# Chunk 2 of a Strassen-style up-projection made paired, and weight splits ahead of the bank work in the down-projection

## Chip, cores and metric

One core of one Trainium2 chip. The metric is the device time of one execution in microseconds (us); lower is better. The kernel before was timed in three runs, and one further execution was profiled.

## What is computed

A decoder layer on 512 tokens of width 2048: attention groups and an output projection, then a feed-forward part. The change touches only the feed-forward part:

```python
def conv_glu_ffn(h, w_up, conv_w, conv_b, w_down):
    u = h @ w_up                                   # (512, 2048) @ (2048, 11264)
    c = conv_general_dilated(u, conv_w, ...) + conv_b   # causal, depthwise, width 3
    gate, val = jnp.split(c, 2, axis=-1)
    return (jax.nn.gelu(gate, approximate=True) * val) @ w_down   # (5632, 2048)
```

All matrices are float32. A RMS norm stands before and after, and the result is added to x.

## The kernel before

**Products in two parts.** Every operand is split into a high part (rounded to float32r, by ScalarE: `hp_to_hi`, `half_to_hi`, `item_to_hi`) and a low part (operand minus high part, by VectorE: `hp_to_lo`, `item_to_lo`, L1884 and L1899). TensorE adds hi x hi, hi x lo and lo x hi in PSUM.

**Up-projection.** The product is done by a seven-product scheme (Strassen-Winograd): the tokens and the inner dimension are halved, gate and value columns are the two halves of the third. The 5632 columns of each half are handled in 22 chunks of 256. Each chunk has seven products P1, P2, P6, P5, P7, P3, P4 (in that order), each in two halves f of 128 columns, so 14 half products, each of 8 k-tiles. `SEQ` lists them; half product w uses slot w % 4 of the split weights `hp_hi` and `hp_lo`. The right operands are quarters of w_up (B11, B12, B21, B22) and their sums T1 = B11 + B12, T2 = T1 + B22, T3 = B12 + B22, T4 = T2 + B21 (signs are taken up elsewhere). P6 takes T2, P5 takes T1, P7 takes T3, P4 takes T4.

**Unpaired and paired chunks.** In an unpaired chunk TensorE issues three 256-wide matmuls for each k (`three_more`, L2509). In a paired one (`two`, L2503) the left operand's high and low parts lie side by side and stream as one 512-wide matmul against the weights' high part; a 256-wide matmul with the low part follows. A paired chunk fills banks 512 wide, so ScalarE's copies out of them (`snap_paired`) are twice as wide, and VectorE must add the two halves (`fold`, and `c12`). Chunks 3 to 20 are paired (`PAIRED`, L77).

**Who makes the sums.** Where a chunk is unpaired, VectorE adds all of T1 to T4 (`make_t`, L1602); T1 and T2 of chunk 2 are made at the last two half products of chunk 1, T3 and T4 in chunk 2. From `PAIRED[0]` on, POOL (GpSimd) issues three adding transfers for each chunk (L1076 to L1088): T1 once the low part of P1's second half is done and B12 has landed, then T3, then T4. VectorE makes T2 alone, at the first half product of the chunk, and waits there for T1's transfer. This goes on to the last chunk, 21, although that one is unpaired.

**Around a half product.** After half product (or half step) w, ScalarE and VectorE each run `after(w)` in program order: bank copies or subtractions, the split of weights w + 4 into the slot just freed, then convolution, gelu, product and left sums of the chunk before, a few instructions for each w. SP's queue loads quarters and stores the products of the chunk before (`spill`, `spill_sums`).

**Down-projection.** Four passes over 22 pairs of row blocks of w_down, two half steps for each pair. Passes 0 and 1 have 12 matmuls, 512 wide, in either half step; passes 2 and 3 have 12 and 6. Each pass adds up in its own set of PSUM banks over all its steps. `w_at(v)` (L788) is the last half step but one of pass v. At the pass boundaries the banks are emptied: ScalarE's `keep` (L1348) copies four banks after `w_at(0)` and `w_at(1)` and two after the next half step; VectorE's `sum_f` (L2084) combines banks and copies, six sums after `w_at(v) + 1` and two more (`12c`) later in the same `after`; after `w_at(2)` two sums, then eight. TensorE's `bank_free` (L2572) waits for these copies and sums before it begins a bank again. In the kernel before they stand at the head of `after`, ahead of the weight split. `item_to_hi` and `item_to_lo` split left operands that were stored and loaded back.

**VectorE also makes block sums** of the down-projection's weights (L1918, `sums_a`; L1909, `sums_b` and `sum_t4`), each ahead of a low part in `after`.

Of the kernel before, what the change touches and what calls it, by code (L numbers as in the profile page):

```python
# [73 lines left out]
CHUNKS = FT // 2  # L74
N_PROD = 7
HPS = 2 * N_PROD
PAIRED = range(3, CHUNKS - 1)  # L77
H_DOWN = CHUNKS * HPS
N_PAIRS = FT // 2
N_PASS = 4  # L80
# [338 lines left out]
def build(nc, x, mem, rel_bias, w_in, a_sinks, w_mem_kv, w_out, g_mix_post, w_up, w_down, g_ffn_post,  # L419
# [13 lines left out]
    with ExitStack() as ctx:  # L433
# [354 lines left out]
        def w_at(v):  # L788
            return H_DOWN + 2 * N_PAIRS * v + 2 * N_PAIRS - 2
# [302 lines left out]
        def _(act):  # L1092
# [172 lines left out]
            for u in range(U_FFN - 1):  # L1265
                for r in range(4):
# [5 lines left out]
                    if (u, r) in SQUARE_AT:  # L1272
                        what, t = SQUARE_AT[u, r]
# [10 lines left out]
                    n = acc_evacuated(u, r)  # L1284
# [198 lines left out]
            def after(w):  # L1483

                c, p, f = SEQ[w] if w < H_DOWN else (CHUNKS, w % HPS // 2, w % 2)
                s = 2 * p + f
                act.wait_ge(hp_used, w + 1)
                if w in (w_at(0), w_at(1)):
                    for what in ("12", "21"):
                        for m in range(2):  # L1490
                            keep(w == w_at(1), what, m)
                if w in (w_at(0) + 1, w_at(1) + 1):
                    for m in range(2):
                        keep(w == w_at(1) + 1, "11", m)
                if c < CHUNKS:
                    if p in SNAP_OF and not (c == 1 and p == P1):
                        (snap_paired if c in PAIRED else snap)(c, SNAP_OF.index(p), f)
                    if c == 0 and p == P7:
                        snap(1, 0, f)
                if w == 3:  # L1500
                    for pair in TURN_H[1]:
                        h_from_psum(1, pair)
                    hp_to_hi(6)
                    hp_to_hi(7)
                elif 3 < w < H_DOWN - 4:
                    hp_to_hi(w + 4)
                elif w >= H_DOWN - 4:
                    half_to_hi(w + 4 - H_DOWN)
                if w == 4:
                    sum_to_hi(OP_S2, 0)  # L1510
                    sum_to_hi(OP_S2, 1)
                if w == 6:
                    sum_to_hi(OP_S1)
                if w == 7:
                    sum_to_hi(OP_S3)
                if w == 9:
                    sum_to_hi(OP_S4)
                if w == 10:
                    sum_to_hi(OP_A22)
                if w == 11:  # L1520
                    act.wait_ge(left_lo, LEFT_COUNT[-1])
                    for f in range(2):
                        act.wait_ge(c11_done, f + 1)
                        act.activation(u_gate[:, f, 0:HALF_S], snaps[:, 0, f, :], ACT.Copy).then_inc(c11_kept, 1)
                i = conv_at(w, c, s)
                if 0 < c <= CHUNKS:
                    if i == 0:
                        if c == 2:
                            begin_conv(c - 1, 0, 0)
                        begin_conv(c - 1, 0, 1)  # L1530
                    if i in (2, 3):
                        gelu(c - 1, i - 2)
                if c < CHUNKS:
                    if s in (12, 13):
                        begin_conv(c, 1, s - 12)
                    if s == 13 and c != 1:
                        begin_conv(c, 0, 0)
                for i in ITEMS_AT.get(w, []):
                    item_to_hi(i)
                if w >= w_at(2) + 4 and w < w_at(2) + 12 and w % 2 == 0:  # L1540
                    f_square(0, (w - w_at(2) - 4) // 2)

# [39 lines left out]
        def _(dve):  # L1582
# [236 lines left out]
            for u in range(U_FFN - 1):  # L1819
                for r in range(4):  # L1820
# [24 lines left out]
                    n = acc_evacuated(u, r)  # L1845
# [27 lines left out]
                    if U_OUT <= u < U_SPLIT and (u - U_OUT) % 4 == 3:  # L1873
                        c = (u - U_OUT) // 4
# [241 lines left out]
            def after(w):  # L2116
# [1 line left out]
                c, p, f = SEQ[w] if w < H_DOWN else (CHUNKS, w % HPS // 2, w % 2)  # L2118
                s = 2 * p + f
                dve.wait_ge(hp_used, w + 1)  # L2120
                if w == w_at(0) + 1 or w == w_at(1) + 1:
                    for m in range(2):
                        for what in ("12b", "21a", "22a"):
                            sum_f(w == w_at(1) + 1, what, m)
                if w == w_at(2):
                    sum_f(0, "11", 0)
                    sum_f(0, "11", 1)
                if w == w_at(2) + 1:
                    sum_f(0, "21b", 0)
                    sum_f(0, "21b", 1)  # L2130
                if w == 14:
                    make_t(1, "T2")
                if PAIRED[0] <= c < CHUNKS and s == 0:
# [49 lines left out]
                if c < CHUNKS:  # L2183
                    if s == 5 and c < PAIRED[0]:
                        make_t(c, "T4")
                    if c == 1 and s in (12, 13):
                        make_t(c + 1, ("T1", "T2")[s - 12])
                    if c == 2 and s == 0:
                        make_t(c, "T3")
                    if s == (5 if c in PAIRED else 10) and c > 0:  # L2190
                        for half in range(2):
# [7 lines left out]
                for i in ITEMS_AT.get(w, []):  # L2199
                    item_to_lo(i)  # L2200
                if w == w_at(0) + 1 or w == w_at(1) + 1:
                    for m in range(2):
                        sum_f(w == w_at(1) + 1, "12c", m)
                if w == w_at(2) + 1:
                    for m in range(2):
                        for what in ("12", "22", "21"):
                            sum_f(0, what, m)
# [453 lines left out]
```

## Time and profile before

| | |
|---|---|
| median of 3 runs | 2003.32 us (2002.27 to 2005.06) |
| the profiled execution: its time | 2007.25 us |
| its span, first to last instruction | 2005.4 us |
| granted TensorE clock, mean | 0.999 of full speed |
| busy: TensorE, VectorE, ScalarE, POOL | 98%, 74%, 50%, 3% |
| chain that ended last, by engine | TensorE 82%, VectorE 11%, issue 3%, ScalarE 3%, DMA 1% |
| up-projection | 668 us to 1562 us of the span, roughly |
| down-projection | 1562 us to 1987 us, roughly |

The times that the profile gives are positions in the span. A timeline row has start, length, engine, line, operation and tiles, then a count (x2 where two like instructions were merged) and in brackets the idle time before it with what ended it. Matmuls are pipelined: the length of one overlaps the next, and the distance between two starts is what one costs.

### The profile page before, as it was taken

The page shows a single profiled execution, that of the slowest core. Times are in us where ns is not written, and L with a number is a line of the kernel's source. Part 1 is how long each engine was busy: PE and PEld are TensorE (multiplying, and loading weights), DVE is VectorE, ACT ScalarE, POOL GpSimd, SP SyncE. Part 2 cuts the span into 40 slices and gives each one's busy share as a digit, 9 for nine tenths or more (in the row PEclk, how much of TensorE's full clock was granted, in tenths as well). Part 3 has the DMA queues.
Part 4 walks back from the last instruction along what each step waited for, and adds up shares of the span by engine and source line. Part 5 has one row for each costly group of instructions (what it writes and reads, how often), then busy time and mean ns, then how long its engine had stood idle before and what let it go on. Part 6 is the DMA issues. An engine that isn't in the chain of part 4 may idle for free.

```text
span 2005.4 us, 27812 instructions
## 1 busy us (share of the span) xinstructions
PE 1969.9 (98%) x10408; PEld 1678.8 (84%) x10408; DVE 1475.8 (74%) x2046; ACT 1011.8 (50%) x1538; POOL 50.3 (3%) x63
## 2 busy tenths in 40 slices
PE   8999999999999999999999999999999999999997
PEld 6888888888887889888888888888889888887885
DVE  4343544545446999788888888888888998879888
ACT  6442332435435755555555555555555655554454
POOL 0000000000000000000000000000000000000000
PEclk9999999999999999999999999999999999999999
DMA  9463222211646444787777877787777997877685
GB/s 384 150 223 95 93 90 71 77 64 64 252 127 213 165 137 153 192 202 220 213 196 201 232 201 199 205 229 203 197 208 196 308 312 233 293 242 233 203 275 189
DMA packets 229109, 388.03 MB, mean 193 GB/s; under 512 B 11842, under 2 KB 139970, under 8 KB 219120
## 3 DMA queue, kind: packets, MB, share of 16 engines
q1 hardware_dynamic: 219520, 320.19, 47.6%
q0 software_dynamic: 8208, 59.77, 14.8%
q10 hardware_dynamic: 1248, 6.29, 0.8%
q8 instruction: 83, 1.36, 0.3%
q14 instruction: 50, 0.41, 0.1%
HBM read 286.30 MB, written 44.07 MB: 165 GB/s over the span
## 4 chain that ended last, share of the span: by engine, by line
PE 82%; DVE 11%; issue 3%; ACT 3%; DMA 1%; SPq 0%; DVEq 0%; ACTq 0%
PE ring L2505 15%; PE ring L2261 12%; PE ring L2263 12%; PE ring L2262 12%; PE ring L2507 8%; PE side L2505 7%; PE side L2507 3%; DVE w_lo L1897 3%; PE side L2261 2%; PE side L2262 2%; PE side L2263 2%; PE side L2337 1%; PE side L2310 1%; DVE f L2107 1%; PE side L2320 1%
## 5 line engine op out<-in xcount | busy, mean ns | idle before, releaser
L1596 DVE TENSOR_TENSOR w_lo<-raw,w_hi 128x512 fp32r<-128x512 f32 x256 | 169.6, 688 | 270.2 <-ACT w_hi L1115 270.0
L2505 PE MATMUL ring<-s,w_hi 128*128 128x512 f32 x864 | 308.1, 400 | 2.4 <-ACT snaps L1434 2.3
L1897 DVE TENSOR_TENSOR w_lo<-raw,w_hi 128x1024 fp32r<-128x1024 f32 x216 | 253.4, 1173 | 74.5 <-ACT w_hi L1325 55.0
L1897 DVE TENSOR_TENSOR w_lo<-q,w_hi 128x1024 fp32r<-128x1024 f32 x218 | 255.5, 1173 | 46.2 <-ACT w_hi L1325 27.9
L1115 ACT ACTIVATE w_hi<-raw 128x512 fp32r<-128x512 f32 x256 | 151.1, 622 | 197.9 <-PE ring L2263 193.5
L2507 PE MATMUL ring<-s,w_lo 128*128 128x256 f32 x864 | 242.9, 281 | 0.0
L1325 ACT ACTIVATE w_hi<-q 128x1024 fp32r<-128x1024 f32 x176 | 185.0, 1055 | 52.4 <-PE side L2507 46.8
L2505 PE MATMUL ring<-a,w_hi 128*128 128x512 f32 x576 | 204.4, 399 | 0.0
L2261 PE MATMUL ring<-w_hi,act_hi 128*128 128x512 f32 x488 | 192.9, 395 | 9.2 <-DVE w_lo L1596 8.7
L2505 PEld LDWEIGHTS ring<-s,w_hi 128*128 128x128 f32 x864 | 162.4, 188 | 44.8 <-ACT snaps L1434 4.9
L1325 ACT ACTIVATE w_hi<-raw 128x1024 fp32r<-128x1024 f32 x130 | 135.1, 1056 | 114.9 <-DVE raw L1600 78.4
L2262 PE MATMUL ring<-w_lo,act_hi 128*128 128x512 f32 x488 | 190.8, 391 | 0.0
L2263 PE MATMUL ring<-w_hi,act_lo 128*128 128x512 f32 x488 | 190.7, 391 | 0.0
L2507 PEld LDWEIGHTS ring<-s,w_lo 128*128 128x128 f32 x864 | 163.5, 189 | 0.0
L2507 PE MATMUL ring<-a,w_lo 128*128 128x256 f32 x576 | 162.0, 281 | 0.0
L2261 PE MATMUL ring<-act_hi,w_hi 128*128 128x512 f32 x384 | 155.3, 404 | 0.0
L2263 PE MATMUL ring<-act_hi,w_lo 128*128 128x512 f32 x384 | 150.3, 391 | 0.0
L2262 PE MATMUL ring<-act_lo,w_hi 128*128 128x512 f32 x384 | 149.6, 390 | 0.0
L1336 ACT ACTIVATE w_hi<-raw 128x1024 fp32r<-128x1024 f32 x86 | 82.6, 960 | 96.1 <-PE ring L2263 46.4
L1336 ACT ACTIVATE w_hi<-q 128x1024 fp32r<-128x1024 f32 x86 | 82.4, 960 | 96.3 <-PE ring L2263 41.5
L2505 PEld LDWEIGHTS ring<-a,w_hi 128*128 128x128 f32 x576 | 108.3, 188 | 26.8
L2261 PEld LDWEIGHTS ring<-w_hi,act_hi 128*128 128x128 f32 x488 | 92.1, 189 | 29.7 <-issue 8.5
(329 smaller groups left out, 4359.5 us busy)
## 6 DMA issues: line engine op xcount, KB each, us to landing
q<-in_w_up SPq DMA_DIRECT2D x65, 1024.0 KB, 5.6
raw<-in_w_in SPq DMA_DIRECT2D x24, 1024.0 KB, 5.2
raw<-in_w_up SPq DMA_DIRECT2D x23, 1024.0 KB, 8.1
q<-q POOLq DMA_DIRECT2D x19, 1024.0 KB, 6.9
q<-raw POOLq DMA_DIRECT2D x19, 1024.0 KB, 6.9
raw<-q POOLq DMA_DIRECT2D x19, 1024.0 KB, 7.3
q<-in_w_down SPq DMA_DIRECT2D x66, 256.0 KB, 4.7
raw<-in_w_down SPq DMA_DIRECT2D x66, 256.0 KB, 4.5
```

The lines of the kernel that those rows point to most:

```text
L1115: act.activation(w_hi[:, s, r * QTR:(r + 1) * QTR], raw[:, s, r * QTR:(r + 1) * QTR], ACT.Copy).then_inc(hi_done, 1)
L1325: act.activation(hp_hi[:, h % 4, :].rearrange("p (k n) -> p k n", n=P), hp_source(h), ACT.Copy, scale=-1.0 if p == P1 else 1.0).then_inc(h ...
L1336: act.activation(half_at(e)[0], half_source(e), ACT.Copy).then_inc(hp_hi_done, 1)
L1596: dve.tensor_tensor(w_lo[:, s, q], raw[:, s, q], w_hi[:, s, q].bitcast(F32), ALU.subtract).then_inc(lo_done, 1)
L1897: dve.tensor_tensor(lo, src, hi.bitcast(F32), ALU.subtract).then_inc(hp_lo_done, 1)
L2107: dve.tensor_tensor(dst, a, b, op).then_inc(f_summed, 1)
L2261: pe.matmul(dst, a_hi_, b_hi_, start=first, stop=False)
L2262: pe.matmul(dst, a_hi_, b_lo_, start=False, stop=False)
L2263: return pe.matmul(dst, a_lo_, b_hi_, start=False, stop=last)
L2310: pe.matmul(score_ps[score_bank(n)][:, 0:nk * P], q_place(n), keys[:, k0 * P:(k0 + nk) * P], start=True, stop=True).then_inc(scores_ready, 1)
L2505: pe.matmul(bank.rearrange("p (h n) -> p h n", h=2), b_hi, hi_lo, start=first, stop=False, skip_group_check=True)
L2507: return pe.matmul(bank[:, 0:HALF_S], b_lo, hi_lo[:, 0, :], start=False, stop=last, skip_group_check=True)
```

## The change

Chunk 2 joins the paired chunks, so its T1, T3 and T4 are made by POOL's transfers, and VectorE makes only its T2, at its first half product. In the down-projection, ScalarE's copies out of the banks (`keep`) and VectorE's sums (`sum_f`) move from the head of `after` to behind the split of the next weights and the left operands.

```diff
-PAIRED = range(3, CHUNKS - 1)
+PAIRED = range(2, CHUNKS - 1)
...
@@ ScalarE, after(w)
                 act.wait_ge(hp_used, w + 1)
-                if w in (w_at(0), w_at(1)):
-                    for what in ("12", "21"):
-                        for m in range(2):
-                            keep(w == w_at(1), what, m)
-                if w in (w_at(0) + 1, w_at(1) + 1):
-                    for m in range(2):
-                        keep(w == w_at(1) + 1, "11", m)
                 if c < CHUNKS:
...
                 for i in ITEMS_AT.get(w, []):
                     item_to_hi(i)
+                if w in (w_at(0), w_at(1)):
+                    for what in ("12", "21"):
+                        for m in range(2):
+                            keep(w == w_at(1), what, m)
+                if w in (w_at(0) + 1, w_at(1) + 1):
+                    for m in range(2):
+                        keep(w == w_at(1) + 1, "11", m)
...
@@ VectorE, after(w)
                 dve.wait_ge(hp_used, w + 1)
-                if w == w_at(0) + 1 or w == w_at(1) + 1:
-                    for m in range(2):
-                        for what in ("12b", "21a", "22a"):
-                            sum_f(w == w_at(1) + 1, what, m)
-                if w == w_at(2):
-                    sum_f(0, "11", 0)
-                    sum_f(0, "11", 1)
-                if w == w_at(2) + 1:
-                    sum_f(0, "21b", 0)
-                    sum_f(0, "21b", 1)
...
-                    if c == 1 and s in (12, 13):
+                    if c == 1 and s in (12, 13) and c + 1 < PAIRED[0]:
                         make_t(c + 1, ("T1", "T2")[s - 12])
-                    if c == 2 and s == 0:
+                    if c == 2 and s == 0 and c < PAIRED[0]:
                         make_t(c, "T3")
...
                 for i in ITEMS_AT.get(w, []):
                     item_to_lo(i)
                 if w == w_at(0) + 1 or w == w_at(1) + 1:
+                    n = w == w_at(1) + 1
                     for m in range(2):
-                        sum_f(w == w_at(1) + 1, "12c", m)
+                        for what in ("12b", "21a", "22a"):
+                            sum_f(n, what, m)
+                    sum_f(n, "12c", 0)
+                    sum_f(n, "12c", 1)
+                if w == w_at(2):
+                    sum_f(0, "11", 0)
+                    sum_f(0, "11", 1)
                 if w == w_at(2) + 1:
+                    sum_f(0, "21b", 0)
+                    sum_f(0, "21b", 1)
                     for m in range(2):
                         for what in ("12", "22", "21"):
                             sum_f(0, what, m)
```

## Rows read from the trace of the kernel before

**Rows 1.** The page: TensorE's busy time, and its granted clock in 40 slices.

```profile
PE 1969.9 (98%) x10408; PEld 1678.8 (84%) x10408; DVE 1475.8 (74%) x2046; ACT 1011.8 (50%) x1538; POOL 50.3 (3%) x63
...
PEclk9999999999999999999999999999999999999999
```

**Rows 2.** TensorE's waits: released by; us in total, times, longest us.

```profile
PE side L2261 <- DVE w_lo L1897: 3.4, 3, 1.3
PE ring L2505 <- ACT snaps L1434: 2.3, 6, 0.8
...
PE side L2261 <- DVE f L2107: 0.8, 1, 0.8
```

**Rows 3.** TensorE's timeline: chunk 2's start and wait, starts of chunks 3, 4, 21.

```profile
764.33 0.28 PE L2511 MATMUL ring<-a,w_hi 128*128 128x256 f32 x1
764.45 0.28 PE L2512 MATMUL ring<-a,w_hi 128*128 128x256 f32 x1
...
781.49 0.28 PE L2513 MATMUL ring<-s,w_lo 128*128 128x256 f32 x1
781.98 0.38 PE L2511 MATMUL ring<-s,w_hi 128*128 128x256 f32 x1 [0.21 <-ACT snaps L1455]
...
805.11 0.40 PE L2505 MATMUL ring<-a,w_hi 128*128 128x512 f32 x1
...
844.68 0.40 PE L2505 MATMUL ring<-a,w_hi 128*128 128x512 f32 x1
...
1521.90 0.28 PE L2511 MATMUL ring<-a,w_hi 128*128 128x256 f32 x1
```

**Rows 4.** VectorE's timeline: P1's second low parts (chunks 2, 3), T2 and P6.

```profile
761.45 1.22 DVE L1894 SCALAR_TENSOR_TENSOR w_lo<-q,w_hi 128x1024 fp32r<-128x1024 f32 x1
...
800.99 1.23 DVE L1894 SCALAR_TENSOR_TENSOR w_lo<-q,w_hi 128x1024 fp32r<-128x1024 f32 x1 [0.99 <-ACT w_hi L1325]
...
809.81 2.29 DVE L1600 TENSOR_TENSOR raw<-raw,q 128x2048 f32<-128x2048 f32 x1 [1.74 <-DMA q<-q]
813.29 1.23 DVE L1897 TENSOR_TENSOR w_lo<-raw,w_hi 128x1024 fp32r<-128x1024 f32 x1 [1.19 <-ACT w_hi L1325]
```

**Rows 5.** T1's transfers (line 1079), and a window: busy by engine, clock, DMA, GB/s.

```profile
DMA to landing us min/median/max: 6.8/6.9/8.0
...
764.00:768.00 4.00, 4.00 (x36) 4.00 (x35) 4.00 (x5) 2.86 (x4) 0.00 (x0) 1.00 0.39 137
```

**Rows 6.** Timelines at the first pass boundary: ScalarE, VectorE, TensorE.

```profile
1680.08 1.09 ACT L1352 ACTIVATE f<-side 128x512 f32<-128x512 f32 x2 [1.61 <-PE ring L2263]
...
1682.00 1.08 ACT L1336 ACTIVATE w_hi<-raw 128x1024 fp32r<-128x1024 f32 x1
...
1684.33 0.68 DVE L2107 TENSOR_TENSOR f<-side,f 128x512 f32<-128x512 f32 x1
...
1688.18 1.22 DVE L1918 TENSOR_TENSOR q<-q 128x1024 f32<-128x1024 f32 x1
...
1688.32 0.51 PE L2261 MATMUL side<-w_hi,act_lo 128*128 128x512 f32 x1 [0.80 <-DVE f L2107]
```

**Rows 7.** The same at the second pass boundary.

```profile
1800.89 1.09 ACT L1352 ACTIVATE f<-side 128x512 f32<-128x512 f32 x2 [2.04 <-PE ring L2263]
...
1804.50 1.10 ACT L1352 ACTIVATE f<-ring 128x512 f32<-128x512 f32 x2
...
1805.94 0.69 DVE L2107 TENSOR_TENSOR f<-side,f 128x512 f32<-128x512 f32 x1
...
1812.79 1.22 DVE L1897 TENSOR_TENSOR w_lo<-raw,w_hi 128x1024 fp32r<-128x1024 f32 x1
...
1814.07 0.50 PE L2261 MATMUL side<-w_hi,d_tok 128*128 128x512 f32 x1 [1.29 <-DVE w_lo L1897]
```

**Rows 8.** The same at the third: VectorE, TensorE.

```profile
1894.64 1.29 DVE L2107 TENSOR_TENSOR f<-ring,f 128x512 f32<-128x512 f32 x2 [0.51 <-PE ring L2263]
...
1905.45 0.50 PE L2261 MATMUL side<-w_hi,d_tok 128*128 128x512 f32 x1 [1.31 <-DVE w_lo L1897]
```

## The prediction

> **What bounds the kernel now.** I read the page first, then TensorE's waits, and last the timeline around each place that the diff touches. The page puts TensorE at 98% busy, and its granted clock stands in the top tenth in all forty slices [rows 1], so it runs at its level of 2.4 GHz. What counts is therefore how fast TensorE can issue, and where it stands still. Its standstills in the FFN are few [rows 2]: 2.3 us in six waits for ScalarE's bank copies (paired chunks), 3.4 us in three waits for weights' low parts, and 0.8 us in one wait for a bank sum (both in the down-projection). The change can win only what these rows and the streams themselves hold. A measurement of this kernel can tell about 0.2%, 4.0 us, from no change.
>
> **Part 1: chunk 2 becomes paired.** The streams. An unpaired half product issues 8 times three 256-wide matmuls, a start every 0.12 us (764.33 to 764.45), so 0.36 us for each k. A paired one issues a 512-wide and a 256-wide matmul. A chunk has 14 half products of 8 k, 112 in all. Unpaired that is 112 x 0.36 = 40.32 us. Paired, chunk 3 ran from 805.11 to 844.68, 39.57 us or 0.3533 for each k [rows 3]. Gain 0.75 us.
> By the Trainium skill (TensorE: Matmul & The Clock Gate, Back-to-back issue gap) a warm matmul of N columns follows its predecessor after N/2.4 + 2.5 ns. Its estimate would be 327.5 ns against 324.9 ns for each k, a gain of 0.3 us, and the total would come out 0.5 us higher. The rows disagree with it (120 ns where it says 109), and the sum goes by the rows.
>
> The wait inside chunk 2. TensorE stood at 781.49 to 781.98, 0.37 us over its pitch, for a bank copy, and the restart cost 0.1 more. The whole chunk took 805.11 - 764.33 = 40.78 us, 1.21 more than chunk 3. I take all **1.21** off: the first paired chunk of the trace had hardly a wait.
>
> What the later chunks do. The 18 paired chunks took (1521.90 - 805.11) / 18 = 39.82 us each, 0.25 over the clean one [rows 3]. Chunk 3 moves from first paired to second, so I give it the mean: **+0.25** (ends 0 and 0.9, the longest wait of that kind in rows 2 with its restart).
>
> The sums by transfers. VectorE loses T1, T3 and T4 of chunk 2, three times 2.29 us [rows 4]. It gains 256 columns more in six subtractions, six folds and two additions of halves, which I put at zero to 7 us of VectorE by the 0.68 us of a 512-wide pass [rows 6]. No wait of rows 2 for VectorE lies in an up-projection chunk of either kind, so both are worth nothing on the path. ScalarE's six bank copies go from 256 to 512 wide; chunk 3 carries the same and did not wait. If that cover fails, the price is the 0.25 just booked.
>
> What is new on the path is T1's transfer. POOL issues it once the second half of chunk 2's P1 has its low part. VectorE waits for it to make T2, T2 is split by ScalarE and VectorE, and then TensorE takes it as P6. Behind T2 in VectorE's order stand that split and the conv taps of chunk 1; behind the transfer in POOL's queue stand T3's and T4's. In chunk 3 this chain is in the rows [rows 4]: trigger at 800.99, T2 begins at 809.81 (8.82 later, 1.74 of it idle for the DMA), the low part of P6's weights begins at 813.29 (3.48 later) and lasts 1.23. Together 13.53 us. In chunk 2 the trigger stands at 761.45, so the weights are ready at 774.98. TensorE comes to P6 after four half products, 764.33 + 32 x 0.3533 = 775.64. Slack: 0.65 us. In chunk 3 the trigger came 4.1 us before the chunk, here 2.9, so the slack is thinner than anywhere in the trace. Against it: the stores of chunk 0's products run between 764 and 768, a DMA share of 0.39 of 4 us, which is 1.56 us of all engines [rows 5], while in chunk 3 the queues were empty. And one of 19 such transfers took 8.0 us where the median took 6.9 [rows 5], 1.1 more. So the stall lies between 0 and 1.56 + 1.1 - 0.65 = 2.0 us; queueing in full without the slow transfer gives 0.9, none gives 0. I take **+0.4**, between those two, as the stores overlap only the transfer's front.
> The Trainium skill (DMA: Bandwidth & Descriptors, Anatomy of one DMA) gives a POOL-issued transfer as 2.0 us + bytes / 436e3, estimated 4.4 us for this megabyte; with it the stall would be 0 and the total 0.4 us lower. The trace's median for the adding transfer is 6.9, so the rule is not followed here.
>
> Removing T1 and T2 from the end of chunk 1 relieves VectorE there, where no row shows TensorE waiting: 0. The loads of chunks 3 and 4 that waited for T4 now wait for the transfer, as in chunk 3, and there it hurt nothing: 0.
>
> **Part 2: weights before the sums, at three pass boundaries.** Call S the last half step but one of a pass. ScalarE's order after S was four bank copies, weights, two copies, weights; it becomes weights, four copies, weights, two copies. VectorE's sums (0.6 to 0.65 us each) move behind one block sum and one low part.
> First boundary [rows 6]: today ScalarE copies from 1680.08 and splits at 1682.00, VectorE's six sums run from 1684.33 to 1688.18, and TensorE restarts at 1688.32. It waits for the last of those sums, not for weights. In the new order the first split and the four copies end at 1680.08 + 0.95 + 1.92 = 1682.95, the next split starts there, its low part starts 1.2 later and lasts 1.2, and the sums begin at 1685.3. The block sum fits in idle time. All is 1.0 later: **+1.0**.
> Second boundary [rows 7]: from 1805.94 VectorE works without a gap through six sums, a block sum and a low part (1.2), two more sums and a block sum up to the low part at 1812.79, for which TensorE restarts at 1814.07. In the new order ScalarE's second split starts at 1804.50 (the last two copies' present place), its 512-wide low part ends at about 1805.75, and what follows is the chain without those 1.2 us: 6.85 - 1.2 = 5.65. The low part begins at 1805.75 + 5.65 = 1811.4, **-1.4**. The first bank copy now ends 0.95 + 0.74 + 0.49 = 2.2 us after S, behind the split and the part of a left operand that stands between 1800.89 and 1804.50; TensorE comes to that bank a half step after S, 12 matmuls or 2.7 us: hidden, with 0.5 to spare, and a cost of the difference if an item more stood there.
> Third boundary [rows 8]: VectorE works without a gap from 1894.64, S's end, to TensorE's restart at 1905.45. The amount of work stays, but in the new order the first thing after one 0.6 us block sum is a low part that ScalarE delivers 1.2 after S: 0.6 us of idle enters a full chain, **+0.6**. The bank sums it pushes back make TensorE wait earlier instead.
> Together +0.2. Ends: -4.2 if the two last waits of rows 2 go altogether (3.4 + 0.8), +1.6 if the second boundary gives nothing. I take the worked-out value. SP's loads wait for low parts, which come earlier, or 0.6 later at the third. But the block sum that now stands ahead of the bank sums needs its blocks up to 5.4 us sooner (1688.18 becomes 1682.8), and no row of mine shows them landed; VectorE would stand in that wait with low part and sums queued behind it. I price it at 0 and put the rest into (b).
>
> **Sum.** -1.21 + 0.25 + 0.4 + 0.2 = **-0.4 us**. The profiled execution took 2007.25 us (span 2005.4 and 1.85 around it), so it would take 2006.9. It lies 3.9 above the median of the runs, 2003.32, and against that I forecast **2002.9**.
>
> **Rivals.**
> (a) Slower: T1's transfer is late. Place: P6 of chunk 2; it decides once T1 lands more than 0.65 us later than in chunk 3's rhythm. With the full 2.0 us: -1.21 + 0.25 + 2.0 + 0.2 = +1.2, 2004.5. For: the thin slack and the stores. Against: the stores begin over 2 us after the trigger, and they fill only 0.39 of their window. 0.2.
> (b) The sums behind the weights cost at the first and third boundary and give nothing at the second, because its block sum waits there for a load that came in time only for the old place: -1.21 + 0.25 + 0.4 + 1.6 = +1.0, 2004.4. For: the first boundary's wait is for a sum. Against: VectorE's gapless chain at the second. 0.13.
> (c) Faster: the boundary waits all go, -4.8, 1998.6. For: the long waits name low parts. Against: VectorE's work between S and the restart hardly shrinks. 0.05.
> My forecast has 0.58; 0.04 is for what no row shows.
>
> **Range.** From the forecast down with no T1 stall (0.4), no waits in chunk 3 (0.25) and one boundary wait gone (1.3), less about 0.7 for the scatter of a median (runs: 2002.27 to 2005.06): 2000.2. Upward (a) with the same scatter: 2005.2. All cases but (c) and a part of the unseen stay within 4.0 us: same 0.91, faster 0.05, slower 0.04.
>
> **What would show it.** Chunk 2 should take about 40.0 us on TensorE, with three POOL transfers in it; T2 waiting 1 to 3 us for the DMA, and the step is wrong if TensorE waits over 1 us at P6. The wait at the first boundary should grow to about 1.8 us for a sum, the second should keep one wait of about 1 us, and the third should split into two short ones. I am wrong altogether if chunk 2 does not shorten, or if the waits of rows 2 go without others in their place.

## The result, and the profile after

The changed kernel is slower, by a little: 2007.64 us median (2004.61 to 2011.28, 20 runs) against 2004.12 us (2001.54 to 2006.64, 20 runs) for the kernel before. The ratio is 1.0019 with a 95% interval of 1.0013 to 1.0025. The forecast was 2002.9 with a range of 2000.2 to 2005.2, so it was wrong in direction and outside the range: -0.4 us was forecast as the change and +3.5 came (a further 0.8 of the distance is that 20 runs of the kernel before have a higher median than the three of the forecast). The profiled execution took 2009.72 us, 2.5 more than the one of before.

The page of the changed kernel, the lines that answer to [rows 1], and one from its part on DMA queues (packets, MB, share of 16 engines):

```profile
span 2007.9 us, 27595 instructions
PE 1969.7 (98%) x10296; PEld 1672.9 (83%) x10296; DVE 1474.7 (73%) x2051; ACT 1013.8 (50%) x1538; POOL 52.9 (3%) x66
...
PEclk9999999999999999999999999999999999999999
...
q8 instruction: 82, 1.34, 0.3%
```

The clock is granted in full as before, and TensorE has 112 matmuls fewer. The time is not in its work but between it. TensorE's waits of the changed kernel, first in the up-projection's chunks from 2 on, then in the down-projection (us in total, times, longest):

```profile
PE ring L2504 <- ACT snaps L1434: 6.9, 7, 2.0
PE ring L2504 <- DVE w_lo L1897: 0.5, 3, 0.2
...
PE side L2260 <- DVE w_lo L1897: 1.5, 2, 1.0
PE side L2260 <- DVE f L2107: 1.4, 2, 1.0
PE ring L2260 <- DVE f L2107: 1.2, 2, 0.8
PE ring L2260 <- DVE w_lo L1897: 0.3, 1, 0.3
```

Against [rows 2] the waits for bank copies grew from 2.3 us to 6.9, while those of the down-projection went from 5.3 (1.1 of it in two waits that are not among the rows shown) to 4.4. TensorE's lines carry a number one lower than before, and one or more higher in some of the kernels below. So the loss lies in the up-projection. Stretches of the changed kernel there, each from one chunk's first matmul to the next chunk's: chunks 2, 3, 6 and 8 (length, then busy time by engine, clock, DMA share, GB/s):

```profile
764.74:807.16 42.42, 40.17 (x227) 34.31 (x225) 33.26 (x42) 22.36 (x29) 2.61 (x3) 1.00 0.80 214
807.16:848.37 41.21, 39.65 (x226) 34.25 (x225) 33.70 (x44) 21.72 (x28) 2.59 (x3) 1.00 0.76 201
928.15:967.72 39.57, 39.57 (x226) 34.30 (x225) 33.83 (x44) 21.73 (x28) 2.59 (x3) 1.00 0.79 210
1007.29:1048.93 41.64, 39.99 (x227) 34.28 (x226) 33.83 (x44) 21.72 (x28) 2.59 (x3) 1.00 0.75 200
```

The kernel before, chunks 2, 3 and 8:

```profile
764.33:805.11 40.78, 40.57 (x339) 40.37 (x338) 36.53 (x40) 21.28 (x29) 1.02 (x1) 1.00 0.44 146
805.11:844.68 39.57, 39.57 (x227) 34.33 (x226) 32.06 (x41) 21.72 (x28) 2.61 (x3) 1.00 0.79 210
...
1004.32:1044.37 40.05, 39.82 (x226) 34.35 (x225) 33.84 (x44) 21.72 (x28) 2.61 (x3) 1.00 0.77 207
```

A clean chunk with wide operands takes 39.57 us in both. Chunk 2 became 1.6 us longer instead of 0.8 shorter. More striking, chunks 3, 8 and 13 (39.98 to 40.66), whose code the diff does not touch, lost 1.6, 1.6 and 0.7, and chunks 6, 7, 12 and 17, which took 40.1 to 40.7, are now clean. The balance is 2.8 us from chunk 2's start to the up-projection's last matmul (797.8 to 800.6 us). One profiled execution of each kernel is compared here, and executions differ: `down_only` below has the same instructions as the kernel before up to the end of the up-projection and took 795.7 us for this stretch, with chunks 7, 12 and 17 at 39.7, 39.6 and 39.6. What comes back from trace to trace is chunk 2 (42.42 us here, 42.44 in `up_only`, 42.60 in `after_pad224`) and chunk 8 (40.1 us in both traces with the stream of before, 41.6 in the changed kernel, `up_only` and `sums_by_vector`).

**Where TensorE's wait in chunk 2 comes from.** The changed kernel's timeline around chunk 2, by engine (VectorE, POOL, VectorE, ScalarE, TensorE):

```profile
761.88 1.22 DVE L1894 SCALAR_TENSOR_TENSOR w_lo<-q,w_hi 128x1024 fp32r<-128x1024 f32 x1
...
763.41 1.01 POOL L1079 DMA_DIRECT2D q<-q  x1 [761.95 <-DVE w_lo L1894]
...
771.59 2.29 DVE L1600 TENSOR_TENSOR raw<-raw,q 128x2048 f32<-128x2048 f32 x1 [3.49 <-DMA q<-q]
775.07 1.22 DVE L1897 TENSOR_TENSOR w_lo<-raw,w_hi 128x1024 fp32r<-128x1024 f32 x1 [1.19 <-ACT w_hi L1325]
777.98 1.23 DVE L1897 TENSOR_TENSOR w_lo<-raw,w_hi 128x1024 fp32r<-128x1024 f32 x1 [1.69 <-ACT w_hi L1325]
...
781.71 0.74 DVE L2059 SCALAR_TENSOR_TENSOR c_gate<-u_gate,conv,c_gate 128x511 f32<-128x511 f32 x1
782.49 0.75 DVE L2062 SCALAR_TENSOR_TENSOR c_gate<-u_gate,conv,c_gate 128x510 f32<-128x510 f32 x1
...
783.27 0.63 ACT L1411 ACTIVATE c_gate<-c_gate 128x512 f32<-128x512 f32 x1 [1.00 <-DVE c_gate L2062]
783.81 0.58 ACT L1434 ACTIVATE snaps<-ring 128x512 f32<-128x512 f32 x1
...
776.44 0.47 PE L2504 MATMUL ring<-s,w_hi 128*128 128x512 f32 x1 [0.23 <-DVE w_lo L1897]
...
784.44 0.50 PE L2504 MATMUL ring<-s,w_hi 128*128 128x512 f32 x1 [2.02 <-ACT snaps L1434]
```

Read upward from the last row. TensorE stands for 2.02 us at product P5, until ScalarE has copied the bank of P6 (783.81). That copy stands in ScalarE's order behind the second gelu of chunk 1 (783.27), which waited 1.00 us for VectorE's taps (781.71, 782.49). The taps stand behind the low parts of P6's weights (775.07, 777.98), these behind T2 (771.59), and T2 waited 3.49 us for T1's transfer (763.41). The row at 776.44 is the wait that I had priced: TensorE at P6, 0.23 us for the low part, 0.4 us with the restart, which is what I had put down. The 2.02 us at P5, some 2.3 us with the restart, are another branch of the same chain: the late transfer reaches TensorE a second time, through T2, the low parts and the taps on VectorE, then the gelu and the copy on ScalarE.

**Why T1 is late in chunks 3 and 8.** POOL's issues of T1 and T3 in the changed kernel, in chunk 3 and in a clean chunk; T3 (L1083) is issued as soon as T1 has landed:

```profile
804.73 0.89 POOL L1079 DMA_DIRECT2D q<-q  x1 [24.37 <-DVE w_lo L1894]
814.40 0.87 POOL L1083 DMA_DIRECT2D q<-raw  x1 [8.79 <-DMA q<-q]
...
886.15 0.86 POOL L1079 DMA_DIRECT2D q<-q  x1 [24.30 <-DVE w_lo L1894]
893.58 0.86 POOL L1083 DMA_DIRECT2D q<-raw  x1 [6.57 <-DMA q<-q]
```

From issue to issue it is 9.67 us in the one and 7.43 in the other. What moved between these moments, by the DMA view of the changed kernel (804.73 to 814.40, then 886.15 to 893.58):

```profile
q0 software_dynamic: 144, 1.05, 52.9%
q8 instruction: 1, 0.02, 0.6%
...
q0 software_dynamic: 144, 1.05, 68.4%
```

The same 144 packets in both, and in the slow one a single packet of instructions. I compared the T1 transfers of all thirteen traces (the kernels before and after and the eleven below), except those of chunk 2, beside which stores run. In 149 of them no packet of the two instruction queues, q8 and q14, started between the issue and the next issue: all took 7.39 to 7.65 us. In the other 98 one did: 7.40 to 9.71 us. No transfer over 7.65 was without one. Queue q8 holds TensorE's instructions: a kernel below with 1029 instructions more on TensorE alone has 4 packets more on it. One such packet comes for every 257 or so of TensorE's instructions, that is at a place set by counting. The change takes 224 instructions out of chunk 2 and so moves every later packet of q8. Not all the chunks that changed follow q8: in chunk 6 of the kernel before T1 took 8.11 us with a packet of q14 alone beside it.

The packets' own times say more about the longest ones. Such a transfer is 128 packets of 8 KB and, at its end, 16 of 4 bytes. In 24 transfers a packet of q8 started 6.9 to 7.1 us behind the issue. In 17 of them it started no earlier than the last of the 4-byte packets, and they took 7.55 to 8.24 us. In the other seven the last 4-byte packet started as the 16 KB packet ended (7.9 to 8.1 us behind the issue, within 0.02 us of that end), and they took 9.61 to 9.71. Chunk 3 of the changed kernel is one of the seven: fetch from 7.07 to 8.05, last packet at 8.04 where a clean transfer has it at 6.49.

The down-projection's three boundaries in the changed kernel, TensorE's restarts that answer to [rows 6 to 8]:

```profile
1690.59 0.50 PE L2260 MATMUL side<-w_hi,act_lo 128*128 128x512 f32 x1 [0.48 <-DVE f L2107]
1692.51 0.50 PE L2260 MATMUL side<-w_hi,act_lo 128*128 128x512 f32 x1 [0.96 <-DVE f L2107]
...
1816.92 0.50 PE L2260 MATMUL side<-w_hi,d_tok 128*128 128x512 f32 x1 [0.99 <-DVE w_lo L1897]
...
1900.54 0.50 PE L2260 MATMUL ring<-w_hi,d_res 128*128 128x512 f32 x1 [0.34 <-DVE f L2107]
1903.03 0.47 PE L2260 MATMUL ring<-w_hi,d_res 128*128 128x512 f32 x1 [0.84 <-DVE f L2107]
```

### The profile page after: what moved, and what is told of

It is laid out like the page before. It is cut to its first block, busy times and chain, and to the rows that moved or that the text cites. A ratio compares the mean times of both kernels' runs of the same rounds, so it can differ in the third digit from the quotient of the medians.

```text
span 2007.9 us, 27595 instructions
## 1 busy us (share of the span) xinstructions
PE 1969.7 (98%) x10296; PEld 1672.9 (83%) x10296; DVE 1474.7 (73%) x2051; ACT 1013.8 (50%) x1538; POOL 52.9 (3%) x66
## 3 DMA queue, kind: packets, MB, share of 16 engines
q8 instruction: 82, 1.34, 0.3%
## 4 chain that ended last, share of the span: by engine, by line
PE 83%; DVE 10%; ACT 3%; issue 2%; DMA 2%; DVEq 0%; ACTq 0%; SPq 0%
PE ring L2504 15%; PE ring L2260 12%; PE ring L2262 12%; PE ring L2261 12%; PE ring L2506 8%; PE side L2504 7%; PE side L2506 3%; DVE w_lo L1897 3%; PE side L2260 2%; PE side L2261 2%; PE side L2262 2%; PE side L2336 1%; PE side L2309 1%; DMA q<-q 1%; DVE f L2107 1%
## 5 line engine op out<-in xcount | busy, mean ns | idle before, releaser
L2504 PE MATMUL ring<-s,w_hi 128*128 128x512 f32 x912 | 324.6, 399 | 7.4 <-ACT snaps L1434 6.9
L2506 PE MATMUL ring<-s,w_lo 128*128 128x256 f32 x912 | 255.9, 281 | 0.0
L2504 PE MATMUL ring<-a,w_hi 128*128 128x512 f32 x608 | 215.3, 398 | 0.0
L2504 PEld LDWEIGHTS ring<-s,w_hi 128*128 128x128 f32 x912 | 171.3, 188 | 52.6 <-ACT snaps L1434 10.0
L2506 PEld LDWEIGHTS ring<-s,w_lo 128*128 128x128 f32 x912 | 172.2, 189 | 0.0
L2506 PE MATMUL ring<-a,w_lo 128*128 128x256 f32 x608 | 170.6, 281 | 0.0
L2504 PEld LDWEIGHTS ring<-a,w_hi 128*128 128x128 f32 x608 | 114.2, 188 | 28.2
```

The lines of the kernel that those rows point to most:

```text
L2504: pe.matmul(bank.rearrange("p (h n) -> p h n", h=2), b_hi, hi_lo, start=first, stop=False, skip_group_check=True)
L2506: return pe.matmul(bank[:, 0:HALF_S], b_lo, hi_lo[:, 0, :], start=False, stop=last, skip_group_check=True)
```

## The experiments

**Which half.** `up_only` is the kernel before with chunk 2's edits alone:

```
-PAIRED = range(3, CHUNKS - 1)
+PAIRED = range(2, CHUNKS - 1)
...
-                    if c == 1 and s in (12, 13):
+                    if c == 1 and s in (12, 13) and c + 1 < PAIRED[0]:
-                    if c == 2 and s == 0:
+                    if c == 2 and s == 0 and c < PAIRED[0]:
```

> The kernel before with the up-projection's part of the change alone (chunk 2 paired, its T1, T3, T4 by transfers). Theory A (the loss is T1's transfer, which comes late for chunk 2 and holds up VectorE's taps, ScalarE's gelu and with it the copy of P6's bank): nearly the whole loss, +2.5 to +4 us against before, with chunk 2 at 41.5 to 42.5 us. Rival C (the loss is in the down-projection's new order): 0 to +1 us here. Rival B (the wider copies and folds are what is late): also +2.5 to +4, told apart by the kernel with the sums on VectorE.

It took 2007.21 us (ratio 1.0016, interval 1.0007 to 1.0025). Its chunks 2, 3 and 8 took 42.44, 41.66 and 41.63 us, and its waits for bank copies, 6.8 us in seven, the longest 2.0, are those of the changed kernel.

`down_only` is the rest of the diff (the keeps and sums behind the weights).

> The kernel before with the down-projection's part of the change alone (weights ahead of the bank work). Theory A: the same as before within 0.5 us, the waits being +1.0, -1.4 and +0.5 us at the three pass boundaries as in the trace after. Rival C: +2.5 to +4 us.

2004.69 us, ratio 1.0003 (0.9994 to 1.0012). Its chunks 2, 3 and 8 take 40.80, 39.57 and 40.06 us, as before. It cannot be told from the kernel before, and `up_only` can: the loss that the runs resolve is in the first half.

**Chunk 2's sums back on VectorE.** In `sums_by_vector` chunk 2 keeps wide operands, and T1 to T4 of it are made by VectorE; POOL starts with chunk 3:

```
+BY_DMA = 3
-            for c in range(PAIRED[0], CHUNKS):
+            for c in range(BY_DMA, CHUNKS):
```

> The kernel after, but chunk 2's T1 to T4 are made by VectorE where they were before (T1 and T2 at the end of chunk 1); chunk 2 stays paired and the transfers begin with chunk 3. Theory A: no wait at P5 of chunk 2, which takes 39.6 to 39.9 us; in all 1 us under before and 4 to 5 us under after. Rival B (wider copies and folds): chunk 2 keeps a wait of about 2 us, and the time stays near after's.

2006.57 us, ratio 1.0015 (1.0006 to 1.0023): the gain did not come. Chunk 2 took 40.72 us and not the 39.6 to 39.9 expected, with one wait of 0.8 us for the copy: VectorE's own T3 stands ahead of the taps here. It lost the wait of 2 us, so wide copies and folds are not what made that one; they stand in every clean chunk of 39.57 us too. And chunk 3, with the first transfer, took 42.61:

```profile
PE ring L2505 <- ACT snaps L1435: 4.9, 5, 1.5
PE ring L2505 <- DVE w_lo L1898: 1.1, 1, 1.1
```

The lateness moved on by one chunk: chunk 3's T1 was issued 0.7 us before the chunk's start, where 2.3 to 2.6 is usual, and took 8.92 us, with a packet of q8 in it. Chunk 8 stayed at 41.59, so its trouble does not come from who makes chunk 2's sums.

**The link through the gelu.** `gelu_later` is the changed kernel with ScalarE's two gelus one product later, so that a gelu that waits for its taps no longer stands ahead of P6's copy:

```
-                    if i in (2, 3):
-                        gelu(c - 1, i - 2)
+                    if i in (3, 4):
+                        gelu(c - 1, i - 3)
```

> The kernel after with ScalarE's two gelus one half product later (behind the copy of P6's first bank instead of ahead of it). Theory A (the link from T1 to TensorE runs through the second gelu): the waits at P5 go in chunks 2 to 20 except for what still reaches the first gelu; every chunk near 39.6 us, the up-projection 5 to 7 us shorter than after's, and the whole 4 to 7 us under after, 1 to 3 under before. A rival in which T1 holds up TensorE by the weights of P6 alone: nothing changes, within 0.5 us of after.

2003.45 us, ratio 0.9994 (0.9985 to 1.0003), about 4 us under the changed kernel. No wait for a copy is left; where T1 is late, P6 itself waits for its weights (chunk 3 still takes 41.15 us, chunk 2 only 40.35):

```profile
PE ring L2504 <- DVE w_lo L1897: 3.2, 6, 1.4
```

`before_gelu_later` makes the same edit in the kernel before.

> The kernel before with ScalarE's two gelus of a chunk one product later. The chain that I hold for the lost time is: late T1, late weights of product 6, VectorE's taps of the convolution behind them, ScalarE's second gelu behind the taps, the copy of TensorE's bank behind the gelu, TensorE at product 5. In this kernel a gelu that waits no longer stands ahead of that copy, so the excess of chunks 4, 6, 7, 8, 12, 13, 17 and 18 (3.4 us in all over 39.57) should go down to under 1 us: 2000.5 to 2002.0 us. If the excess was not in this link but in the weights of product 6 themselves: 2004.1 us.

2002.57 us, ratio 0.9990 (0.9981 to 0.9999), 0.6 us above the range that I gave. In the profile the 18 chunks from 3 to 20 take 39.57 us each, with no wait at all. The windows view over them:

```profile
805.36:1517.68 712.32, 712.32 (x4035) 617.73 (x4033) 606.82 (x772) 395.35 (x504) 46.81 (x54) 1.00 0.79 209
```

The kernel before took 716.79 us for them [rows 3: 805.11 to 1521.90], so the link cost 4.5 us in that execution already, and 2.4 in that of `down_only` (714.73 us). The ratio of the times says 2 us.

**The chain's slack, directly.** `late_t1` is the kernel before with POOL waiting for the weights of P2's first bank:

```
-                pool.wait_ge(hp_lo_done, place(c, P1, 1) + 1)
+                pool.wait_ge(hp_lo_done, place(c, P2, 0) + 1)
```

> The kernel before with T1's start delayed: POOL waits for VectorE's weights of product 2's first bank in place of product 1's second, about 2.6 us later. By the chain through the taps, the gelu and the bank's copy, whose slack is 0.15 to 0.35 us, TensorE pays nearly all of it at product 5: each of the 18 chunks with wide operands grows from 39.57 to about 41.8 us, some 40 us in all, 2044 us. By the slack of 1.9 us that my prediction read at product 6's weights it would pay only 0.7 us per chunk, some 13 us in all, 2017 us.

2051.98 us in one run, past the 2044 expected by the chain through the copy and far from the 2017 of the other. The 18 chunks took 758.85 us, 42.16 each, where a clean one takes 39.57: 2.6 us of delay cost 2.6 on average, and 2.0 to 2.6 in the 13 chunks whose T1 took 7.4 to 7.6 us. In chunk 5, T2 waits 3.40 us for the transfer, and TensorE pays at two places, P6's weights and P6's copy. First TensorE's waits of this kernel, then the two restarts of that chunk:

```profile
PE ring L2505 <- ACT snaps L1434: 24.9, 17, 1.5
PE ring L2505 <- DVE w_lo L1897: 16.1, 18, 2.0
...
904.04 0.47 PE L2505 MATMUL ring<-s,w_hi 128*128 128x512 f32 x1 [0.48 <-DVE w_lo L1897]
911.33 0.50 PE L2505 MATMUL ring<-s,w_hi 128*128 128x512 f32 x1 [1.50 <-ACT snaps L1434]
```

The weights alone had some 2 us of slack (0.5 of 2.6 reaches TensorE there), the copy next to none.

**The place of the fetches.** Two kernels shift TensorE's stream and nothing else. `before_pad32` and `after_pad224` put 32 and 224 increments of an unused semaphore first on TensorE:

```
+            for _ in range(32):
+                pe.nop().then_inc(pad, 1)
             pe.wait_ge(ident_ready, 2)
```

> The kernel before, with 32 semaphore increments that nobody waits for as TensorE's first instructions, in its 7 us of idle time before the first matmul; nothing else differs. The theory under test: the 16 KB of instructions that TensorE's fetch queue brings every 250 or so of its instructions lengthen chunk's first adding transfer (T1) when they fall into it, from 7.4-7.6 us to 8-9.7 us, and the change, by issuing 224 instructions fewer in chunk 2 (32 more, in steps of 256), moved these fetches from chunks 6, 7, 12 and 17 into chunks 3, 8 and 13. It expects this kernel, whose work is the kernel before's, to have the changed kernel's lengths from chunk 3 on: chunks 3, 8 and 13 at about 41.2, 41.6 and 40.7 us, chunks 6, 7 and 12 at 39.6, and a time of 2005.0 to 2006.5 us. The rival, that the longer chunks 3, 8 and 13 follow from what the change does in chunk 2 (wide operands there, its sums late): the chunks stay as in the kernel before (39.6, 40.1 and 40.0 us), 2004.1 us.

The profile sides with the theory at chunk 8, and in part at chunk 3. Its stretches for both:

```profile
805.21:845.27 40.06, 39.83 (x227) 34.29 (x225) 32.07 (x41) 21.72 (x28) 2.61 (x3) 1.00 0.78 207
...
1004.31:1045.51 41.20, 39.66 (x227) 34.08 (x225) 33.74 (x44) 21.73 (x28) 2.60 (x3) 1.00 0.75 202
```

Chunk 8 went from 40.05 to 41.20. Chunks 7, 12 and 17 went from 40.2, 40.7 and 40.2 to 39.6, 39.6 and 39.2, but that proves little, as `down_only` has them at 39.6 to 39.7 without a shift. Chunk 3 reached 40.06 and not 41.2, chunk 13 stayed at 40.05, and chunk 6 at 40.08. Chunk 8's T1 took 9.64 us here and chunk 3's 8.20, where the changed kernel has 9.66 and 9.67: the packet falls into both, at about the same moment, but in chunk 3 it stands behind the transfer's last packet and in chunk 8 before it. The time was 2006.95 us (2006.84 without one run of 3278.4 us; ratio 1.0011, 1.0002 to 1.0020), slower than before as expected and even 0.45 above the range. The profiled execution does not show this loss: at 2004.86 us it was below that of before (2007.25), and its up-projection took 797.0 us from chunk 2's start, against 797.8 and 795.7. What 32 increments cost in the median I therefore take from the ratio.

> The changed kernel with 224 such increments in front, as many instructions as the change took away. By the theory of the fetches chunks 3 and 8 go back from 41.2 and 41.6 us to 39.6-39.9 and 40.1, chunk 13 from 40.7 to 40.0, chunks 6, 7 and 12 grow to 40.1-40.7, and chunk 2 alone stays above its length before: 2005.5 to 2006.5 us, 1 to 2 us under the changed kernel. By the rival (a state that chunk 2 leaves behind) chunks 3 and 8 stay long: 2007.6 us.

2035.21 us. This increment is dear: the first matmul starts at 35.3 us instead of 7.0, and chunk 2 at 793.29, 28.6 later. Behind that the chunks that the theory wanted clean are clean: 3 and 8, shown here, and 13 (39.64). Of those that should grow 7 did (40.12) and 17 with it (40.67), while 6 and 12 stayed at 39.6. Chunks 2, 3 and 8:

```profile
793.29:835.89 42.60, 40.15 (x226) 34.26 (x225) 33.23 (x42) 22.34 (x29) 2.61 (x3) 1.00 0.79 213
835.89:875.47 39.58, 39.58 (x226) 34.33 (x225) 33.84 (x44) 21.73 (x28) 2.59 (x3) 1.00 0.79 209
1034.34:1073.96 39.62, 39.51 (x226) 34.28 (x225) 33.89 (x44) 21.73 (x28) 2.59 (x3) 1.00 0.78 210
```

Chunk 3 is clean although chunk 2 is as late as in the changed kernel, so its late chunk 2 alone does not make chunk 3 late. From chunk 2's start to the last matmul of the up-projection it is 796.9 us, against 800.6 for the changed kernel and 797.8 for the kernel before. Of the 2035.21, less the 28.6 in front, 2006.6 is left; the profile of this kernel gains 3.7 us in the chunks, its median, so reckoned, 1.0.

**Fetches locked in place.** A chunk with wide operands issues 462 TensorE instructions (448 matmuls and weight loads, 14 waits). 50 satisfied waits more make it 512, twice 256, so that each chunk should find the fetches where the last one did (1029 instructions for 4 packets is 257 for each); 79 instructions in front choose the place. `locked` does so on `gelu_later`:

```
+                    if c in PAIRED and k in (1, 3, 5, 7)[:4 if h % HPS < 8 else 3]:
+                        pe.wait_ge(ident_ready, 1)
+                        pe.wait_ge(ident_ready, 2)
                     if c in PAIRED:
                         mm = two(
```

> The changed kernel with the later gelus, and 50 satisfied waits added to each chunk with wide operands, so that a chunk has 512 TensorE instructions and every fetch comes at the same place of each chunk, about 10 and 30 us after its start, never within T1's transfer (79 increments in front place it). By the theory of the fetches every T1 takes 7.4-7.6 us from chunk 3 on, and if the added waits cost TensorE nothing, each of these chunks takes 39.3-39.6 us: 1999 to 2001.5 us. What a wait costs in TensorE's stream no row shows; at 0.05 us each exposed it would be 2.5 us per chunk, some 48 us in all. If fetches are not the cause, T1's times vary as before (7.4 to 9.7 us).

2006.97 us (1.0014, 1.0005 to 1.0023), because the 79 increments in front cost 6.5 us at the start, which I had not reckoned with. Behind them every T1 from chunk 3 on took 7.46 to 7.75 us, and the chunks 39.57 to 39.73. The 50 waits cost TensorE nothing in these chunks. The fetches came about 18 and 35 us after a chunk's start and not at 10 and 30; T1 is issued about 37 us after it, so they fell outside the transfer, some of them by 1 us only.

`after_locked` is the changed kernel with the same lock and its gelus where they were, and the 79 as waits among the mixer's wide matmuls.

> The changed kernel (its gelus where they were) with the fetches locked as in the run 'locked': 50 satisfied waits more per chunk with wide operands, and the 79 instructions in front of them now waits among the wide matmuls of the mixer's projections, so that nothing is lost at the start. By the theory of the fetches T1 takes 7.4-7.7 us in every chunk from 3 on, chunks 3, 8 and 13 fall from 41.2, 41.6 and 40.7 to 39.6-39.8 us, and only chunk 2 (40.8 to 42.4) stays long: the last matmul of the up-projection at 1560.5 to 1562.5 instead of 1565.3, and 2002.5 to 2005.0 us. If the later gelus, and not the place of the fetches, had cleaned the chunks in 'locked', chunks 3 and 8 stay over 40.5 us here and the time stays near 2007.

2003.63 us, ratio 1.0000 (0.9991 to 1.0009), with the last matmul of the up-projection at 1559.4, 1.1 earlier than my range. Chunks 2, 3 and 8 in it, its waits for copies, POOL's T1 and T3 in chunk 3 and the DMA queues between them:

```profile
764.80:806.77 41.97, 39.73 (x226) 34.07 (x225) 33.11 (x42) 22.34 (x29) 2.61 (x3) 1.00 0.81 217
806.77:846.29 39.52, 39.52 (x226) 34.14 (x225) 33.89 (x44) 21.73 (x28) 2.60 (x3) 1.00 0.79 210
1005.07:1044.65 39.58, 39.58 (x227) 34.34 (x225) 33.84 (x44) 21.73 (x28) 2.59 (x3) 1.00 0.79 210
...
PE ring L2509 <- ACT snaps L1434: 2.3, 2, 2.0
...
804.45 0.89 POOL L1079 DMA_DIRECT2D q<-q  x1 [24.05 <-DVE w_lo L1894]
811.90 0.87 POOL L1083 DMA_DIRECT2D q<-raw  x1 [6.57 <-DMA q<-q]
```

7.45 us between the issues where the changed kernel has 9.67, with every instruction of VectorE, ScalarE and POOL the same. The two waits for copies that are left are chunk 2's and a short one of chunk 4, whose T1 took 8.2 us with a packet of the other instruction queue in it. Moving the fetches alone took some 4 us off the changed kernel's time. How much of its loss against the kernel before they are is not measured: no run locks the kernel before, which pays for fetches too.

`gelu_locked` has both edits.

> The same with the later gelus too. In 'locked' its 20 chunks took 792.8 us, with 6.5 us lost in front; without that loss the last matmul of the up-projection stands at 1557 to 1558, as in the kernel before with the later gelus: 2000.5 to 2003 us, 4 to 6 us under the changed kernel. If the added waits among the projections cost something there, the start of chunk 2 shows it (764.7 in the changed kernel).

2001.23 us (2000.51 to 2002.59, 11 runs), ratio 0.9984 (0.9975 to 0.9993): the lowest median of all, and faster than both kernels; from `before_gelu_later` (0.9981 to 0.9999) the runs do not tell it apart. The up-projection's last matmul is at 1558.0, at the upper end of what I gave. Chunk 2 takes 40.35 us, and the others are clean.

Its profiled span, 1999.7, is that of `before_gelu_later`, 1999.6. Once no chunk waits, wide operands in chunk 2 bring nothing that this can tell.

## Why the prediction was wrong

**Chunk 2 (-1.21 + 0.4).** The streams were right: TensorE's busy time in chunk 2 is 40.17 us with its restarts, and a clean chunk 39.57. (The 120 ns for 256 columns do not speak against the Trainium skill as the prediction has it. Its page TensorE: Matmul & The Clock Gate, Back-to-back issue gap, gives N/2.4 + 2.5 ns for a matmul by itself and says that it counts too little, at few columns, in a stream where each matmul has its weight load; here there are 10408 of either [rows 1].) But I took off the wait of chunk 2 as well and booked a new one at +0.4; the chunk became 1.64 longer, 2.4 over -1.21 + 0.4.

What I followed, I had right. The trigger of T1, the low part of P1's second half, stands at 761.88, 2.9 us before the chunk as forecast (2.9). The transfer took 8.6 us from issue to next issue, 0.9 over the one of chunk 3 from which the chain was read, T2 began 9.7 us behind the trigger instead of 8.8, and less the slack of 0.65 that leaves 0.25 us of stall at P6. It was 0.23, and 0.4 with the restart; that I had taken just 0.4 out of 0 to 2.0 was in part luck. The transfer takes 8.6 to 8.8 us in every kernel here that has it. Whether that is the stores' doing, as I had priced it, is not shown: two packets of q14 stand in each of these transfers as well, and no run separates them.

The step that failed is the end of the chain. "Behind T2 in VectorE's order stand that split and the conv taps of chunk 1": I named them, did not follow them, and so put their delay at nothing. They carry the gelu, and behind the gelu stands P6's bank copy, whose slack is next to none where I had found 0.65 us at P6 (`late_t1`: 2.6 us late, 2.6 us lost per chunk; `gelu_later`: with the copy ahead of the gelu chunk 2 falls from 42.42 to 40.35). My mark "wrong if TensorE waits over 1 us at P6" looked at the wrong product; it waited 2.02 at P5. The reason why the engines' added load was "worth nothing on the path", that no wait of rows 2 names VectorE in these chunks, does not hold either: the waits for ScalarE's copies were the end of a chain through VectorE, as `before_gelu_later` shows, in which none is left.

**The later chunks (+0.25).** They took 1.2 us more in the profile. I let chunk 3 have the mean excess and left the others as they were. In fact nine chunks changed by over 0.3 us, from -1.1 to +1.6; but those of chunks 7, 12 and 17 are about what two executions of one stream differ by (`down_only`). I read the excess of single chunks (0 to 1.1) as noise with a mean. A part of it was a pattern with a period of five chunks: 5 x 462 = 2310 = 9 x 256 + 6 instructions. Nothing in the diff's text says that 224 instructions fewer move it; I had rows for the spread, one of 19 transfers at 8.0 us where 6.9 was usual [rows 5], and did not ask what was different about that one.

**The down-projection (+0.2).** Right, point by point. Predicted +1.0, -1.4, +0.6; with the restarts, the waits went from 1.10 to 2.04, from 2.64 to 1.29 and from 1.60 to about 2.05: +0.94, -1.35, +0.45. The first boundary now has two waits for sums, the second one of about 1 us, the third two short ones of 0.3 and 0.8 us and one of 0.1. So the sum is about 0, and the time of `down_only` agrees with that as far as its interval (-0.06% to +0.12%) can tell.

**The rivals.** (a), T1's transfer late, had the right cause, but its path to TensorE was wrong: the price at P6, which (a) put at up to 2.0, was 0.4, and the rest came at P5. (b) and (c) did not occur. The range failed because its upper end took the unknown of one stall (2.0) and none for chunks that the diff leaves alone.

What stays open: the longest transfers are 2.2 us over a clean one, and the last packet, held up behind the fetch, accounts for about 1.5 of it; why the landing follows that packet later too, and what decides which of the two goes first, no run shows. Chunk 3's excess is 1.64 us with a late chunk 2 and the packet, 0.49 with the packet alone (`before_pad32`), 0.01 with a late chunk 2 alone (`after_pad224`).

## What to carry to other kernels

Follow a late transfer through the engines' orders, past the instruction that reads it: what stands behind its reader, and what behind that, until TensorE is reached on every branch; the least slack may lie on a branch that never touches the data. Where several like stages differ for no visible reason, take that as a lead and line each one up with everything in the trace that is periodic, the instruction queues included. And when such a kernel is compared with a version that issues more or fewer instructions, a tenth or two of a per cent may be the shift alone: move the stream by a few satisfied waits and look whether the difference stays. Profile a kernel twice before reading single stages: one stream of instructions gave 716.8 and 714.7 us here for the same 18 chunks.

## What the hardware showed that I had not expected

- TensorE's instructions arrive over the same 16 DMA engines, in packets of 16 KB (1.34 MB in 82), one per 257 or so instructions. The packet takes 0.6% of 16 engines over 9.67 us, 0.9 us of one engine, but the adding transfer beside it lasts up to 2.2 us longer. The Trainium skill (DMA: Bandwidth & Descriptors, SWDGE vs HWDGE vs iDMA) has an engine take its 16 internal queues in turn. By that alone T1's share of this engine would wait for about the packet's own 0.9 us. The trace agrees in part: in seven transfers T1's last packet started as the 16 KB packet ended, 1.0 us after its start. But they landed later by more than that, and no run here says why.
- An increment of an unused semaphore costs TensorE 0.16 us as one of its first instructions (224 of them, first matmul at 35.3 us); 32 vanish in the 7.2 us for which it waits there anyway. Satisfied waits among matmuls cost nothing here: with 50 more per chunk a chunk takes 39.57 us as without.
- A 256-wide matmul with its own weight load starts every 0.12 us, with the clock in full [rows 3]; 2 us of stall in TensorE's stream added no drop of the granted clock (1.00 in every stretch shown).
